# One comparison for four plain one-hots, and GpSimd in the routing stage of a PEER decoder step

## The reference

```
q = (xb @ w_q).reshape(PEER_BLOCK, P_HEADS, 2, P_HALF)
s = einsum('thpd,hpkd->thpk', q, sub_keys)
s1, i1 = top_k(s[:, :, 0], 16);  s2, i2 = top_k(s[:, :, 1], 16)
cand = s1[..., :, None] + s2[..., None, :]
cidx = i1[..., :, None] * 128 + i2[..., None, :]
top, pos = top_k(cand, 16);  idx = take_along_axis(cidx, pos)
g = softmax(top)
act = gelu(einsum('td,thkd->thk', xb, u[idx]))
out = einsum('thk,thkd->td', g * act, v[idx])
```

## Time and profile before

| what | value |
|---|---|
| median of 3 runs | 2789.27 us (2789.21 to 2790.97) |
| profiled execution, first to last instruction (its own time) | 2791.7 us |
| mean granted TensorE clock | 0.958 |
| routing stage of layer 0, first to last weigh | 746.8 to 882.7 us |
| routing stage of layer 1, first weigh to start of the last | 2259.6 to 2394.8 us |

### The profile page before, as it was taken

One profiled execution on the slowest core, in us unless ns is written; L12 is line 12 of the kernel. 1 busy time (PEld: TensorE's weight loads), 2 busy tenths in 40 slices (PEclk: granted clock), 3 DMA queues, 4 the chain that ended last, 5 costly groups with the idle time before them and its releaser, 6 DMA issues. The chain is left out here.

```text
span 2791.7 us, 50744 instructions
## 1 busy us (share of the span) xinstructions
PE 2530.5 (91%) x17672; PEld 2236.5 (80%) x17672; DVE 1823.1 (65%) x3955; ACT 1552.8 (56%) x3124; POOL 263.3 (9%) x240
## 2 busy tenths in 40 slices
PE   6978999999867999997989998899999976899997
PEld 3658988888756999997765534798899975899997
DVE  6844789866798555557244455349885479755555
ACT  5635655676696555556413542255556579555554
POOL 0000444100000000000001110014440000000000
PEclk8989999999988999999989999999999988999999
DMA  6743444577301455553206986344445510355452
GB/s 235 256 135 139 155 162 152 209 251 260 136 0 47 180 181 180 180 181 126 64 30 247 344 327 243 121 162 155 159 164 175 180 59 0 108 179 181 180 180 106
DMA packets 65102, 455.79 MB, mean 163 GB/s; under 512 B 8656, under 2 KB 8864, under 8 KB 10224
## 3 DMA queue, kind: packets, MB, share of 16 engines
q1 hardware_dynamic: 52128, 379.61, 38.5%
q0 software_dynamic: 11120, 73.29, 6.8%
q10 hardware_dynamic: 1760, 1.68, 0.2%
HBM read 415.27 MB, written 39.27 MB: 163 GB/s over the span
## 5 line engine op out<-in xcount | busy, mean ns | idle before, releaser
L824 ACT ACTIVATE w_parts<-ring 128x512 fp32r<-128x512 f32 x1376 | 851.4, 630 | 856.0 <-PE ps L423 767.0
L1199 DVE TENSOR_TENSOR w_parts<-ring,w_parts 128x512 fp32r<-128x512 f32 x1232 | 853.8, 704 | 606.1 <-ACT w_parts L824 597.3
L423 PE MATMUL ps<-h_hi,w_parts 128*128 128x264 f32 x5376 | 1022.7, 289 | 83.3 <-DVE w_parts L1199 58.0
L423 PEld LDWEIGHTS ps<-h_hi,w_parts 128*128 128x128 f32 x5376 | 854.9, 191 | 123.7 <-issue 68.7
L423 PE MATMUL ps<-h_lo,w_parts 128*128 128x264 f32 x2688 | 770.7, 287 | 0.0
L423 PE MATMUL ps<-g_parts,w_parts 128*128 128x264 f32 x6144 | 749.6, 284 | 7.5 <-DVE g_parts L1495 7.5
L423 PEld LDWEIGHTS ps<-g_parts,w_parts 128*128 128x128 f32 x6144 | 749.3, 189 | 7.8 <-issue 7.8
L423 PEld LDWEIGHTS ps<-h_lo,w_parts 128*128 128x128 f32 x2688 | 515.4, 192 | 2.0
L423 PE MATMUL ps<-SCR 128*128 128x128 f32 x1056 | 185.5, 331 | 92.4 <-DVE SCR L1466 85.2
L1126 POOL TENSOR_TENSOR w_parts<-ring,w_parts 128x512 fp32r<-128x512 f32 x144 | 210.9, 1466 | 479.6 <-ACT w_parts L824 479.2
L423 PEld LDWEIGHTS ps<-SCR 128*128 128x128 f32 x1056 | 158.9, 231 | 118.8 <-issue 87.9
(11 more groups left out here) (176 smaller groups left out, 1473.3 us busy)
## 6 DMA issues: line engine op xcount, KB each, us to landing
ring<-in_stream SPq DMA_DIRECT2D x362, 1024.0 KB, 4.8
BIG<-in_C POOLq DMA_DIRECT2D x32, 1024.0 KB, 8.5
out_C_s<-BIG POOLq DMA_DIRECT2D x32, 1024.0 KB, 5.9
out_C_p<-BIG POOLq DMA_DIRECT2D x16, 256.0 KB, 2.3
x<-in_x ACTq DMA_DIRECT2D x1, 1056.0 KB, 15.0
out_y<-BIG POOLq DMA_DIRECT2D x1, 1056.0 KB, 4.2
consts<-in_consts ACTq DMA_DIRECT2D x1, 256.0 KB, 10.4
BIG<-in_gates POOLq DMA_DIRECT2D x1, 192.0 KB, 2.7
```

Source lines behind the costliest of these rows:

```text
L423: return nc.tensor.matmul(out, lhsT, rhs, start=start, stop=stop, skip_group_check=shared)
L824: return nc.scalar.activation(to, of, f, **kw_)
L1199: tt(w_lo[:, j % HALVES, :], half_of(n, half), w_hi[:, j % HALVES, :].bitcast(F32), ALU.subtract).then_inc(lo_ready[half], 1)
```

## The change

VectorE makes all four plain one-hots by one comparison of 512 columns (L1499 of the changed kernel). Of the four weighted ones it makes the last as before (L1503). For the other three (BY_ACT = 3) GpSimd subtracts i from iota for 384 columns at once (the new `differences`, L1151), and ScalarE takes the Abs of that and then, per token, the Relu of (w - w times that), with w and -w as scalars per partition (helper `func`, L829 now). The tile `minus_w` with -w is new; VectorE fills it from the transposed picks (L1492). TensorE writes the product of token i to every fourth column of the bank, from column i on, so that a bank holds for each row of experts the four tokens side by side; `weigh` (L1509) then goes through G row by row, four tokens at a time.

```diff
-        oh_j_abs = [sem(f"oh_j_abs{l}") for l in range(2)]
+        oh_i_apart = [sem(f"oh_i_apart{l}") for l in range(2)]
+        oh_i_abs = [sem(f"oh_i_abs{l}") for l in range(2)]
+        oh_i_act_ready = [sem(f"oh_i_act_ready{l}") for l in range(2)]
...
+                    pe.wait_ge(oh_i_act_ready[l], r * OH + (s + 1))
...
-                        last = mm(ps[:, s, i * P:(i + 1) * P], oh_j[s][:, i, :], oh_i[s][:, i, :])
+                        last = mm(ps[:, s, i:BANK:4], oh_j[s][:, i, :], oh_i[s][:, i, :])
...
-                    for i in range(4):
-                        last = func(oh_j[s][:, i, :], iota, ACT.Abs, scale=-1.0,
-                                    bias=pickT[:, 1, bass.ds(r * (4 * OH) + (4 * s + i), 1)])
-                    last.then_inc(oh_j_abs[l], 1)
-                    act.wait_ge(oh_j_abs[l], r * OH + (s + 1))
-                    func(flat(oh_j[s]), flat(oh_j[s]), ACT.Relu, scale=-1.0, bias=1.0).then_inc(oh_j_ready[l], 1)
+                def apart(g, s):
+                    act.wait_ge(oh_i_apart[l], g + 1)
+                    d = flat(oh_i[s][:, 0:BY_ACT, :])
+                    func(d, d, ACT.Abs).then_inc(oh_i_abs[l], 1)
+
+                def weighted(g, s):
+                    act.wait_ge(oh_i_abs[l], g + 1)
+                    for i in range(BY_ACT):
+                        t = bass.ds(g * 4 + i, 1)
+                        last = func(oh_i[s][:, i, :], oh_i[s][:, i, :], ACT.Relu, scale=minus_w[:, t],
+                                    bias=pickT[:, 2, t])
+                    last.then_inc(oh_i_act_ready[l], 1)
+                act.wait_ge(pickT_ready[l], NB + 1)
+                apart(0, 0)
+                with act.Fori(0, GROUPS // OH) as r:
                     for s in range(OH):
-                        build(r, s)
...
+                        apart(r * OH + (s + 1), (s + 1) % OH)
+                        weighted(r * OH + s, s)
...
+            def differences(l):
+                iota3 = iota.unsqueeze(1).to_broadcast([P, BY_ACT, KEYS])
+                def build(r, s):
+                    if not (isinstance(r, int) and r == 0):
+                        pool.wait_ge(route_done[l], r * OH + (s + 1 - OH))
+                    i3 = pickT[:, 0, bass.ds(r * (4 * OH) + 4 * s, BY_ACT)].unsqueeze(2)\
+                        .to_broadcast([P, BY_ACT, KEYS])
+                    nc.gpsimd.tensor_tensor(oh_i[s][:, 0:BY_ACT, :], iota3, i3, ALU.subtract)\
+                        .then_inc(oh_i_apart[l], 1)
+                pool.wait_ge(pickT_ready[l], NB)
...
             low_rows(0)
+            differences(0)
...
+                dve.wait_ge(pickT_done[l], NB)
                 for b, (t0, nb) in enumerate(BLOCKS):
-                    dve.wait_ge(pickT_done[l], b + 1)
-                    last = vec.tensor_copy(
+                    vec.tensor_copy(
                         pickT[:, :, t0:t0 + nb],
-                        ps[:, 4 + b, 0:3 * P].rearrange("p (i t) -> p i t", i=3)[:, :, 0:nb])
+                        ps[:, 4 + b, 0:3 * P].rearrange("p (i t) -> p i t", i=3)[:, :, 0:nb]).then_inc(pickT_ready[l], 1)
+                    last = ts(minus_w[:, t0:t0 + nb], ps[:, 4 + b, 2 * P:2 * P + nb], -1.0, None, ALU.mult)
...
-                    for i in range(4):
+                    j4 = pickT[:, 1, bass.ds(g * 4, 4)].unsqueeze(2).to_broadcast([P, 4, KEYS])
+                    tt(oh_j[s], iota.unsqueeze(1).to_broadcast([P, 4, KEYS]), j4, ALU.is_equal)\
+                        .then_inc(oh_j_ready[l], 1)
+                    for i in range(BY_ACT, 4):
                         t = bass.ds(g * 4 + i, 1)
                         last = ts(oh_i[s][:, i, :], iota, pickT[:, 0, t], pickT[:, 2, t], ALU.is_equal, ALU.mult)
...
-                    Gt = G[:, :, bass.ds(g * 4, 4)].rearrange("p r t -> p t r")
-                    tt(Gt, ps[:, s, :].rearrange("p (t r) -> p t r", t=4), Gt, ALU.mult).then_inc(routed[l], 1)
+                    Gt = G[:, :, bass.ds(g * 4, 4)]
+                    tt(Gt, ps[:, s, :].rearrange("p (r t) -> p r t", t=4), Gt, ALU.mult).then_inc(routed[l], 1)
```

More of the change, by code:

```diff
@@ L248, in decoder_step @@
         pickT = scr(1152, 3, TOK)
+        minus_w = scr(0, TOK)
         OH = 4
+        BY_ACT = 3
         oh_j = [scr(2048 + i * 1024, 4, KEYS) for i in range(OH)]
@@ L975, in peer @@
                         act.wait_ge(work_free[l], 1)
-                def build(r, s):
-                    if not (isinstance(r, int) and r == 0):
-                        act.wait_ge(route_done[l], r * OH + (s + 1 - OH))
-                    for i in range(4):
-                        last = func(oh_j[s][:, i, :], iota, ACT.Abs, scale=-1.0,
-                                    bias=pickT[:, 1, bass.ds(r * (4 * OH) + (4 * s + i), 1)])
-                    last.then_inc(oh_j_abs[l], 1)
-                    act.wait_ge(oh_j_abs[l], r * OH + (s + 1))
-                    func(flat(oh_j[s]), flat(oh_j[s]), ACT.Relu, scale=-1.0, bias=1.0).then_inc(oh_j_ready[l], 1)
[L987 to L990, removed]
-                    for s in range(OH):
-                        build(r, s)
-                for s in range(GROUPS % OH):
-                    build(GROUPS // OH, s)
+                def apart(g, s):
[12 more added lines that the diff above has]
+                with act.Fori(0, GROUPS // OH) as r:
+                    for s in range(OH):
+                        apart(r * OH + (s + 1), (s + 1) % OH)
+                        weighted(r * OH + s, s)
+                apart(GROUPS - 1, (GROUPS - 1) % OH)
+                weighted(GROUPS - 2, (GROUPS - 2) % OH)
+                weighted(GROUPS - 1, (GROUPS - 1) % OH)
                 act.wait_ge(route_done[l], GROUPS)
@@ L1128, in low_rows @@
                             .then_inc(lo_ready[1], 1)
+            def differences(l):
[8 more added lines that the diff above has]
+                pool.wait_ge(pickT_ready[l], NB)
+                for s in range(OH):
+                    build(0, s)
+                with pool.Fori(1, GROUPS // OH) as r:
+                    for s in range(OH):
+                        build(r, s)
+                for s in range(GROUPS % OH):
+                    build(GROUPS // OH, s)
             pool.wait_ge(hs_ready, NC)
@@ L1166, in _ @@
             low_rows(1)
+            differences(1)
             pool.wait_ge(y_ready, 1)
@@ L1453, in peer @@
                     modulation(1, 0, 6 * NC, 3)
+                dve.wait_ge(pickT_done[l], NB)
                 for b, (t0, nb) in enumerate(BLOCKS):
-                    dve.wait_ge(pickT_done[l], b + 1)
-                    last = vec.tensor_copy(
+                    vec.tensor_copy(
                         pickT[:, :, t0:t0 + nb],
-                        ps[:, 4 + b, 0:3 * P].rearrange("p (i t) -> p i t", i=3)[:, :, 0:nb])
+                        ps[:, 4 + b, 0:3 * P].rearrange("p (i t) -> p i t", i=3)[:, :, 0:nb]).then_inc(pickT_ready[l], 1)
+                    last = ts(minus_w[:, t0:t0 + nb], ps[:, 4 + b, 2 * P:2 * P + nb], -1.0, None, ALU.mult)
                 last.then_inc(pickT_ready[l], 1)
-                dve.wait_ge(pickT_ready[l], 1)
+                dve.wait_ge(pickT_ready[l], NB + 1)
                 def build(g, s):
-                    for i in range(4):
+                    j4 = pickT[:, 1, bass.ds(g * 4, 4)].unsqueeze(2).to_broadcast([P, 4, KEYS])
+                    tt(oh_j[s], iota.unsqueeze(1).to_broadcast([P, 4, KEYS]), j4, ALU.is_equal)\
+                        .then_inc(oh_j_ready[l], 1)
+                    for i in range(BY_ACT, 4):
                         t = bass.ds(g * 4 + i, 1)
```

## The result

The changed kernel takes **2728.44 us** (median of 4 runs, 2727.81 to 2729.83), the kernel before, beside it, 2789.47 (4 runs, 2789.21 to 2790.97): a ratio of 0.9777, 95% interval 0.9764 to 0.9791. In a second comparison it took 2728.31 (5 runs, 0.9769, 0.9756 to 0.9783). The direction was forecast; the gain is 61 us where 33.5 was forecast.

What follows compares the result with a forecast made beforehand. VectorE was taken to bound the routing stage. Cutting its period from 2.077 to 1.79 over 65 periods gains 18.7 us, less 1.9 for the start: 16.8 per layer, 33.5 in all, forecast 2756 us, range 2728 to 2797.

Steps and rivals of the forecast that it cites:

- the chain over GpSimd: Routing period per group at full clock: GpSimd 0.91, comparison 0.55, one-hot 0.26, in all 1.72 us.
- the share of the lower clock: Routing stage: some 29% stays at TensorE's 1.2 GHz, group 2.0 us there, making the mean period 1.79.
- the third rival: VectorE and GpSimd don't delay each other in routing: period 1.48, 1.60 with the lower clock, 2731 us; chance 7%.
- VectorE's own work, 1.48 per group: Routing, per group: comparison 0.61, weigh 0.61 and one one-hot 0.26 us, against 2.03 before.
- GpSimd's price: GpSimd's 128x384 subtraction in routing: taken as 1.05 us, between bounds of 0.97 and 1.30.
- The new wait: GpSimd's and VectorE's two-operand SBUF instructions don't run together; the waiting one ends 0.14 or 0.15 us sooner than its duration alone.
- three Relus at about 0.30 ... 1.5 at most, under 1.72, so hidden: ScalarE per routing group: Abs on 384 columns, 0.39 to 0.63, plus three Relus; 1.5 us at most, not the bound.
- 2.3 later: Start of each routing stage: added multiplications, GpSimd subtractions, Abs and Relus delay it 2.3 us; net 1.9 per layer.
- The first: Rival: writing every fourth column slows TensorE's routing matmuls, period 2.0 at either clock level, 2783 us; chance 13%.
- The second: Rival: GpSimd gets in between VectorE's comparison and one-hot, which stands 0.86 longer; period 2.34, 2827 us, slower; chance 15%.
- The fourth: Rival: GpSimd needs 1.30 us for 384 columns too, routing period 1.97, 2779 us; chance 5%.

Runs made afterwards that it cites:

- interleaving alone: The kernel before with only the interleaved columns (matmul output and weigh as in the change, one-hots as before): 2755.72 us against 2790.68, ratio 0.9869.

## Why the prediction was right in direction and wrong in size

The forecast gain was little more than half of the measured one. Two terms of the sum failed, each worth some 7 us per layer: the period at full clock (1.72 by the chain over GpSimd, measured 1.57) and the share of the lower clock (29% kept, nearly none measured). The start of the stage was mis-sized the other way, 1.9 net per layer for 3.5 measured. That the time still lies at the lower end of the range is luck: that end came from the third rival.

**VectorE's own work, 1.48 per group**: right. It was measured as 1.49, with a weigh of 0.69, a comparison of 0.68 and one one-hot.

**GpSimd's price**: wrong, and with it the chain. I bounded 128x384 by 0.97 and 1.30 from L1126, the only shape of the trace, and took the bounds for safe on both sides; it is 0.83. L1126 subtracts two tiles in full and writes another type (fp32r), this one reads two broadcast operands and writes f32; which of these makes the difference wasn't tried. The trace had no row of this form, and "the nearest row" gives no lower bound. The estimate of 1.03 from the Trainium skill ("GPSIMD Engine Reference", section 3.1) scaled the same row and is as far off.

**The new wait, a chain of 1.72**: its form holds, its size doesn't. The comparison does wait for GpSimd's end (done 0.54 after it, 0.55 forecast) and the one-hot does take part (0.87 beside GpSimd). With 0.83 for 1.05 the same chain gives 0.69 + 0.55 + 0.26 = 1.50, about what VectorE needs for itself, so the chain stopped being a separate bound. Nor does the period show it: GpSimd waits 0.68 to 0.80 per group for TensorE.

**ScalarE, "three Relus at about 0.30 ... 1.5 at most, under 1.72, so hidden"**: wrong in price and in consequence. The 0.30 was an Abs with one scalar per partition; the Relu has two, which makes 479 ns of 388, and 386 once the scale is a constant. With Abs and three Relus, 1.55 to 1.57 a group, ScalarE became a second bound beside VectorE's.

**The lower clock, "if 29% of the time stays there"**: wrong. I took the share as a property of the stage. In the changed kernel's second profile TensorE is at the lower level (1.2 GHz) for the first groups, after its wait at the start (a granted clock of 0.50 from 748 to 752), and at full clock from 760 on:

```profile
744.00:760.00 16.00, 9.24 (x51) 8.30 (x52) 13.61 (x24) 13.17 (x33) 9.02 (x10) 0.79 0.00 1
760.00:840.00 80.00, 59.45 (x416) 49.99 (x414) 79.97 (x155) 80.00 (x206) 43.28 (x52) 1.00 0.00 0
```

Over the kernels the granted clock of 752 to 840 went with the period: 1.00 at 1.83 (interleaving alone), 0.99 at 1.84, 0.76 at 2.25, 0.62 at 2.43. Which of the two drives the other was not separated. Had 29% stayed, my formula would make 1 / (0.71 / 1.57 + 0.29 / 2.0) = 1.675 of a period of 1.57: 65 x 0.105 = 7 us per layer of the 13 that the forecast missed. The chain, 1.72 taken for 1.57, makes another 7.5 (the mean period 1.79 for 1.675), and the later start takes 1.6 of these back.

**The start, "2.3 later"**: 3.9. The multiplications (0.5) and the two subtractions before ScalarE's first Relus (2.1) are there. Not counted: the copies now wait for all transposes and begin 1.20 after the first instead of 0.60, and the first group runs at the lower clock, 2.20 from matmul to weigh instead of 1.28.

**The rivals.** The first (strided output slows TensorE) falls: 1.15 for eight records, and the stage runs at 1.57. The Trainium skill's rule ("PSUM — Partial Sum Buffer", Specifications), that any non-contiguous access slows matmuls significantly, isn't borne out for writing every fourth column here. The second is a real mechanism, but in the loop it shows only where the weigh is long. The third, 2731, gave nearly the measured time by a wrong reason: it has the ports cost nothing (they cost 0.08) and the lower clock stay. The fourth falls with GpSimd's 0.83.

## What to carry to other kernels

When work is spread from one full engine over others, price each new operation by its exact form (how many scalars per partition, which operands), and compare the engines' sums per period with each other: the one counted as hidden was here one of two bounds, 0.01 to 0.02 us apart (1.546 without the subtraction, 1.554 and 1.563 without the Abs). Of two edits to one engine's queue, one can be a loss alone (26 us here) and still make the pair worth more (61) than the other alone (35), so time each alone and both together before keeping or dropping one. And a share of low clock read before a change is not a constant of the stage: it can vanish when the period changes.

## What was unexpected of the hardware

- A second scalar per partition on ScalarE costs 93 ns of 479 (128 columns).
- GpSimd's subtraction with broadcast operands takes 608 ns for 256 columns and 827 for 384, 1.7 ns a column and some 0.17 besides; its one-hot with two scalars takes 787 for 128.
- Writing every fourth column of a bank costs TensorE nothing visible (1.15 for eight records), and going through G in runs of four neighbours makes the weigh 0.69, no more than contiguous operands.
- GpSimd gets in between two instructions of VectorE that stand back to back, if it starts while the first runs: with the weigh of 1.08, 28 of 60 one-hots last 0.84 to 0.94 behind a subtraction that starts 1.02 to 1.65 after the weigh. With the weigh of 0.69 the subtraction of the same group starts beside the weigh or beside the one-hot (815.38 and 816.88 above), and the comparison alone is stretched, by 0.08.
